# Expert sums on TensorE in four 64x64 tiles, two picks at a time, in a two-layer model on one core

## Chip, cores and metric

One of the eight cores of a Trainium2 chip runs the whole program. The metric is the time of one execution in microseconds (us) on the device. TensorE multiplies into PSUM, which has 8 banks of 128 partitions x 512 fp32 numbers; VectorE (DVE), ScalarE (ACT) and GpSimd (POOL) do the rest, and SyncE (SP) issues the stream of weights.

## What is computed

Two blocks over 512 tokens of width 1024. The first has windowed attention and a convolution branch, then PEER: for each token, 8 heads pick 16 of 16384 experts each, and

```python
s_top, i_top = lax.top_k(s, PEER_TOPK)          # per head and key half, then over the 16x16 sums
g = jax.nn.softmax(best, axis=-1)
ue = jnp.take(u_tab, idx, axis=0)               # idx: token, head, pick
ve = jnp.take(v_tab, idx, axis=0)
act = jax.nn.gelu(jnp.einsum('thkd,td->thk', ue, t), approximate=False)
return jnp.einsum('thk,thkd->td', (g * act), ve)
```

So 128 experts are summed for each token, and each has a row of 1024 for the dot product and a row of 1024 for the sum. The second block is two layers: an mLSTM mixer, attention over a memory of 256 rows and a squared-ReLU MLP of 4096; then a pooling mixer, attention and MLP again.

## The kernel before

**Tiles.** Activations lie transposed, features on partitions. A weight tile is 128 output features by 1024, 512 KB, streamed in a ring of four (`RING`). Each is split by ScalarE (`upper_after`) and VectorE (`lower_after`) into an upper and a lower part, and a product is 24 matmuls (three for each of 8 blocks of 128 features, L523 to L525), over 512 tokens or, in the mixer, attention and MLP of layer one, over a half of 256. `SECTIONS` gives for each section its first tile n and first product o.

**Banks.** Product o goes to PSUM bank o modulo 4. The reader of a product adds one to that bank's semaphore (`free`), and TensorE waits for it before product o + 4 (`wait_bank`). Banks 4 and 5 hold sums of squares, means, scores and turned values of the moment; banks 6 and 7 hold the expert sums.

**Picks.** A pick p is one expert for each of 128 tokens; there are 128 picks for each of 4 token blocks, 512 in all. GpSimd gathers its 128 rows of 8 KB (both rows of the expert) into one of up to ten slots (L492); VectorE takes the dot product (`expert_dot`, L2053); ScalarE makes the weight and from it a 128x128 diagonal matrix (`expert_weight`, L1342 to L1351), of which there are two; TensorE multiplies the diagonal with the gathered rows, in fp32, in two halves of 512 columns (`expert_sum`, L771), adding to banks 6 and 7, and frees the slot (`pick_used`). After 128 picks ScalarE copies the two banks out (L1357), TensorE turns them by 8 transposes (`turn_peer`, L780) and VectorE adds them to the residual (`add_peer`, L2062); the next block's first pick waits for that.

**Order.** All engines follow one order that is written out. The first 256 picks (`EARLY`) come with only the memory's 16 products between them. The others are spread over the tiles of the first half: `pick_ends` gives for each tile the number of picks that TensorE has added after it (two a tile, and some more at gaps), and `groups` names the places where several products are computed together, feature block by feature block, with their picks behind them. VectorE's dots run up to two picks ahead (`dot_picks`); ScalarE weighs the picks of a tile before it reads that tile's product (`weigh_picks`).

**A head of the mixer** (`half_lstm_core`): scores (L888), two tiles (the output gate, copied out by ScalarE at L1407) with picks behind each, the denominator (L901, read at L2307), the floor (L906), two value products (L913, read at L2319). `lstm_out` begins four products of the output projection over six of eight feature blocks while the last head is normalised.

## Time and profile before

| | |
|---|---|
| median of 3 runs | 3343.65 us (3343.54 to 3348.61) |
| the profiled execution | 3350.57 us, its span 3348.8 us |
| TensorE busy | 2926.9 us (87%) |
| VectorE, ScalarE, GpSimd busy | 2245.0, 1396.0, 600.2 us |
| gathers (queue q0) | 536.90 MB, 512 picks |
| weight stream | 390 tiles of 512.0 KB |
| picks on TensorE | from 624.9 to 2274.1 us |

A busy TensorE is not TensorE at its peak: a matmul's record runs on while the next has begun, so the time of a matmul is read from start to start. The DMA share is the mean busy share of the core's 16 DMA engines; it can come out a little over one.

### The profile page before, as it was taken

Reading aid. Unit: us, or ns where it says so; the run is one execution under the profiler, and the core shown is the slowest. Engines: PE = TensorE matmul, PEld = TensorE weight load, DVE = VectorE, ACT = ScalarE, POOL = GpSimd, SP = SyncE. Lnnn points to the kernel's source line nnn. Section 1 sums busy time; section 2 is a strip of 40 time slices with the busy share of each in tenths; the row PEclk is TensorE's granted clock in tenths of the full one; section 3 lists DMA queues with packets and bytes.
Section 4 is the critical chain, followed back from the end, with each engine's and each line's share of the span. In section 5 each row is a group of like instructions: output and inputs, shape, how many; then the busy total and the mean of one; then the engine's idle time right before and its main releaser. Section 6 shows DMA issues by size and latency. Waiting matters only on the chain. (4 is left out here: it accounts for less than half of the span.)

```text
span 3348.8 us, 40044 instructions
## 1 busy us (share of the span) xinstructions
PE 2926.9 (87%) x13452; PEld 2098.1 (63%) x13452; DVE 2245.0 (67%) x4588; ACT 1396.0 (42%) x2972; POOL 600.2 (18%) x545
## 2 busy tenths in 40 slices
PE   6999899877888888888889899997888976989998
PEld 6777677422344443556556566666778974778886
DVE  6775554588878886755666776777667777564445
ACT  3346323333444443655444544445544433332222
POOL 0000000233333444331323233330000011000000
PEclk9999899988898898998989999998989987989999
DMA  6531122799999999896868799992224540122221
GB/s 243 197 109 63 38 88 82 281 370 387 384 384 388 414 419 404 333 371 218 319 255 349 309 418 419 418 415 82 87 94 140 189 145 19 57 82 94 92 97 51
DMA packets 142422, 779.05 MB, mean 233 GB/s; under 512 B 15008, under 2 KB 18208, under 8 KB 76448
## 3 DMA queue, kind: packets, MB, share of 16 engines
q0 software_dynamic: 73728, 536.90, 39.8%
q1 hardware_dynamic: 62832, 220.43, 18.8%
q10 hardware_dynamic: 5680, 19.40, 1.6%
q8 instruction: 101, 1.65, 0.2%
q14 instruction: 81, 0.66, 0.1%
HBM read 774.58 MB, written 2.10 MB: 232 GB/s over the span
## 5 line engine op out<-in xcount | busy, mean ns | idle before, releaser
L492 POOL DMA_INDIRECT slots<-in_experts,consts x376 | 419.0, 1114 | 1371.4 <-PE psum L771 725.8
L2053 DVE SCALAR_TENSOR_TENSOR slots<-slots,work 128x1024 f32<-128x1024 f32 x376 | 460.5, 1225 | 236.1 <-DMA slots<-in_experts,consts 217.4
L1685 DVE TENSOR_TENSOR wlo<-w,whi 128x1024 fp32r<-128x1024 f32 x390 | 473.7, 1220 | 140.6 <-ACT whi L1151 139.4
L771 PE MATMUL psum<-slots,acc 128*128 128x512 f32 x824 | 420.6, 663 | 114.6 <-ACT acc L1351 114.6
L1151 ACT ACTIVATE whi<-w 128x1024 fp32r<-128x1024 f32 x390 | 409.1, 1050 | 212.8 <-PE psum L525 212.0
L771 PEld LDWEIGHTS psum<-slots,acc 128*128 128x128 f32 x824 | 167.5, 211 | 351.6 <-issue 188.8
L771 PE MATMUL psum<-slots,consts 128*128 128x512 f32 x680 | 324.9, 622 | 29.8 <-ACT consts L1351 27.2
L1342 ACT ACTIVATE consts<-consts 128x1 f32<-128x1 f32 x512 | 100.8, 197 | 473.5 <-DVE slots L2053 356.6
L523 PE MATMUL psum<-xhi,whi 128*128 128x512 f32 x664 | 268.5, 404 | 1.9 <-DVE wlo L1685 1.9
L523 PE MATMUL psum<-xhi_h,whi 128*128 128x256 f32 x880 | 267.8, 304 | 2.0 <-DVE wlo L1685 2.0
L524 PE MATMUL psum<-xlo,whi 128*128 128x512 f32 x664 | 262.9, 396 | 0.0
L525 PE MATMUL psum<-xhi,wlo 128*128 128x512 f32 x664 | 262.8, 396 | 0.0
L524 PE MATMUL psum<-xlo_h,whi 128*128 128x256 f32 x880 | 248.0, 282 | 0.0
L525 PE MATMUL psum<-xhi_h,wlo 128*128 128x256 f32 x880 | 247.7, 281 | 0.0
L771 PEld LDWEIGHTS psum<-slots,consts 128*128 128x128 f32 x680 | 126.7, 199 | 176.1 <-issue 121.9
L523 PE MATMUL psum<-yhi_h,whi 128*128 128x256 f32 x640 | 195.2, 305 | 4.0 <-DVE ylo_h L2366 4.0
L523 PE MATMUL psum<-yhi,whi 128*128 128x512 f32 (+1 forms) x416 | 170.3, 409 | 31.4 <-POOL ylo L510 21.8
L524 PE MATMUL psum<-ylo_h,whi 128*128 128x256 f32 x640 | 179.3, 280 | 0.0
L525 PE MATMUL psum<-yhi_h,wlo 128*128 128x256 f32 x640 | 179.2, 280 | 0.0
L523 PEld LDWEIGHTS psum<-xhi_h,whi 128*128 128x128 f32 x880 | 168.3, 191 | 12.1 <-issue 7.2
L524 PEld LDWEIGHTS psum<-xlo_h,whi 128*128 128x128 f32 x880 | 168.1, 191 | 9.7 <-issue 9.6
L525 PEld LDWEIGHTS psum<-xhi_h,wlo 128*128 128x128 f32 x880 | 167.9, 191 | 0.0
(336 smaller groups left out, 5884.8 us busy)
## 6 DMA issues: line engine op xcount, KB each, us to landing
w<-in_stream SPq DMA_DIRECT2D x390, 512.0 KB
arena<-in_wmod SPq DMA_DIRECT2D x4, 2048.0 KB, 17.8
arena<-in_wmod ACTq DMA_DIRECT2D x8, 1024.0 KB, 6.7
acc<-in_wmod ACTq DMA_DIRECT2D x8, 1024.0 KB, 8.0
slots<-in_experts,consts POOLq DMA_INDIRECT x376
xres<-in_xT SPq DMA_DIRECT2D x1, 2048.0 KB, 15.1
outT<-xres SPq DMA_DIRECT2D x8, 256.0 KB, 2.0
arena<-in_experts,consts POOLq DMA_INDIRECT x93
```

The lines of the kernel that those rows point to most:

```text
L492: pool.indirect_dma_start(out=slots[slot], out_offset=None, in_=a["experts"], in_offset=bass.IndirectOffsetOnAxis(ap=indices[:, p:p + 1], ...
L523: pe.matmul(dst, hi, xh(k), start=(j == 0), stop=False)
L524: pe.matmul(dst, hi, xl(k), start=False, stop=False)
L525: mm = pe.matmul(dst, lo, xh(k), start=False, stop=(j == len(ks) - 1))
L771: mm = pe.matmul(bank(6 + half), diag(p), v[:, half * T:(half + 1) * T], start=(c == 0), stop=(c == PICKS - 1))
L1151: act.activation(whi[:, s, :, :].rearrange("p k n -> p (k n)"), w32[:, s, :], ACT.Copy)\
L1342: act.activation(gelus[:, c:c + 1], inner[:, c:c + 1], ACT.Gelu).then_inc(sem("gelu_ready"), 1)
L1685: dve.tensor_tensor(wlo[:, s, :, :].rearrange("p k n -> p (k n)"), w32[:, s, :], whi[:, s, :, :].rearrange("p k n -> p (k n)").bitcast(F32 ...
L2053: dve.scalar_tensor_tensor(u, u, 1.0, tokens[:, p // PICKS, :], ALU.mult, ALU.mult, accum_out=inner[:, c:c + 1]).then_inc(sem("dotted"), 1)
```

## The change

Two picks are added together, by eight fp32 matmuls over 64 rows and 64 columns of the array. The diagonal is 128x64 (rows 0 to 63 hold the weights of tokens 0 to 63 on its diagonal, rows 64 to 127 those of the others), and there are four of them. An even pick sends token rows 0 to 63 to PSUM partitions 0 to 63 and rows 64 to 127 to partitions 64 to 127; an odd pick crosses them. Row group r and half h go to bank 4 + 2r + h, so the sums take four banks, and the crossed parts are brought together when the block is turned: 16 fp32 matmuls with two identities of 64 stacked (`pair`) in place of 8 transposes, behind four copies.

Since banks 4 to 7 are taken, the products from the memory's keys up to the second half's mixer use banks 0 and 1 alone (`out_banks`), and what was in banks 4 and 5 goes to 2 and 3 in that time (`side`, `norm_bank`). In the first half, groups of four products become groups of two, and two products of the output projection are begun early, not four. Elsewhere `bank(o % RING)` becomes `out_bank(o)`, the same bank as before. The core of the diff:

```diff
+def out_banks():
+
+    first, last = SECTIONS["memk"][1], SECTIONS["lstm1"][1]
+    banks = [o % (2 if first <= o < last else RING) for o in range(len(DONE))]
+    return banks, [banks[:o].count(b) for o, b in enumerate(banks)]
+
+
+OUT_BANK, OUT_TURN = out_banks()
...
-    groups = {first: 2, SECTIONS["xq0"][0]: 4, SECTIONS["mlp0"][0]: 4}
+    groups = {first: 2, SECTIONS["xq0"][0]: 2, SECTIONS["mlp0"][0]: 2}
...
-        diags = [t.rearrange("p (a n) -> p a n", a=2)
+        diags = [t.rearrange("p (a n) -> p a n", a=4)
                  for t in (flat_acc[:, 512:768], consts[:, _CONST["perm"][0]:_CONST["perm"][0] + 256])]
 
         def diag(p):
-            return diags[p // EARLY][:, p % 2, :]
+            return diags[p // EARLY][:, p % 4, :]
 
...
+        def out_bank(o):
+            return bank(OUT_BANK[o])
+
+        def side(half):
+            return 2 if half == 0 else 4
+
+        def norm_bank(ni):
+            return 2 if 3 <= ni < 7 else 4
...
-            if o >= RING:
-                eng.wait_ge(bank_free[o % RING], o // RING + shift)
+            if OUT_TURN[o]:
+                eng.wait_ge(bank_free[OUT_BANK[o]], OUT_TURN[o] + shift)
...
-                if c == 0:
+                if p % 2 == 0:
+                    return
+                if c == 1:
                     pe.wait_ge(sem("peer_added"), 8 * t) if t else pe.wait_ge(sem("tokens_copied"), 2 * TT)
-                if p == 0:
+                if p == 1:
                     pe.wait_ge(sem("key_scores_copied"), HP)
                 pe.wait_ge(sem("diagonal"), p + 1)
-                v = slots[SLOT[p]][:, D:2 * D]
                 for half in range(2):
-                    mm = pe.matmul(bank(6 + half), diag(p), v[:, half * T:(half + 1) * T], start=(c == 0),
-                                   stop=(c == PICKS - 1))
-                mm.then_inc(sem("pick_used"), 1)
+                    f = slice(D + half * T, D + (half + 1) * T)
+                    for q in (p - 1, p):
+                        for r in range(2):
+                            rows = slice(64 * r, 64 * r + 64)
+                            to = 64 * (r ^ (q % 2))
+                            mm = pe.matmul(psum[to:to + 64, 4 + 2 * r + half, :], diag(q)[rows, :], slots[SLOT[q]][rows, f],
+                                           start=(c == 1), stop=(c == PICKS - 1))
+                        if half:
+                            mm.then_inc(sem("pick_used"), 1)
 
             def turn_peer(t):
 
+                pe.wait_ge(sem("peer_copied"), 4 * t + 4)
                 for half in range(2):
-                    pe.wait_ge(sem("peer_copied"), 2 * t + half + 1)
                     for k in range(4):
-                        mm = pe.transpose(bank(6 + half)[:, k * P:(k + 1) * P],
-                                          peer_tokens(t)[:, half, k * P:(k + 1) * P], ident)
+                        for r in range(2):
+                            f = (4 * half + k) * P
+                            c = k * P + 64 * r
+                            mm = pe.matmul(bank(6 + half)[:, c:c + 64], peer_tokens(t)[:, r, f:f + P], const("pair"),
+                                           start=True, stop=True)
                     mm.then_inc(sem("peer_turned"), 1)
 
-            def turn_copied(m, o, src, tiles, turned):
+            def turn_copied(m, o, src, tiles, turned, at=2):
...
-                lstm_out(0, range(0, 6))
-                lstm_out(1, range(0, 6))
+                begun = 2 * (1 + half)
+                for m in range(begun // 2):
+                    lstm_out(m, range(0, 6))
                 head_sums(3)
-                lstm_out(2, range(0, 6))
+                for m in range(begun // 2, begun - half):
+                    lstm_out(m, range(0, 6))
                 head_spread(3)
-                lstm_out(3, range(0, 6))
-                for m in range(4):
+                for m in range(begun - half, begun):
+                    lstm_out(m, range(0, 6))
+                for m in range(begun):
                     lstm_out(m, range(6, 8))
-                for m in range(4, KB):
...
-                half_linear_group(n, range(o, o + 4), (sem(f"split{4 + 4 * half}"), 0))
+                group = 4 if half else 2
+                half_linear_group(n, range(o, o + group), (sem(f"split{4 + 4 * half}"), 0))
+                sum_picks(n + 1)
                 for m in range(KB):
-                    if m >= 4:
+                    if m >= group:
                         half_linear(n + m, o + m + (0, 0, 0, 0, 1, 1, 2, 2)[m])
...
-                half_linear_group(n, range(o, o + 4), (sem(f"split{5 + 4 * half}"), 0))
-                sum_picks(n + 3)
+                group = 4 if half else 2
+                half_linear_group(n, range(o, o + group), (sem(f"split{5 + 4 * half}"), 0))
+                sum_picks(n + 1)
+                for m in range(group, 4):
...
-                if p >= 2:
-                    act.wait_ge(sem("pick_used"), p - 1)
-                act.activation(diag(p), ident, ACT.Copy, scale=weights[:, c:c + 1])\
+                if p >= 4:
+                    act.wait_ge(sem("pick_used"), p - 3)
+                act.activation(diag(p), const("pair"), ACT.Copy, scale=weights[:, c:c + 1])\
...
                 act.wait_ge(sem("pick_used"), PICKS * (t + 1))
-                for half in range(2):
-                    act.activation(peer_tokens(t)[:, half, :], bank(6 + half), ACT.Copy).then_inc(sem("peer_copied"), 1)
-
-            def turn_back(m, dst, tiles, turned):
+                for r in range(2):
+                    for half in range(2):
+                        act.activation(peer_tokens(t)[:, r, half * T:(half + 1) * T], bank(4 + 2 * r + half), ACT.Copy)\
...
+    parts["pair"] = np.tile(np.eye(64), (2, 1))
```

## Rows read from the trace of the kernel before

**Rows 1.** The page: the span, and the DMA share in 40 slices.

```profile
span 3348.8 us, 40044 instructions
...
DMA  6531122799999999896868799992224540122221
```

**Rows 2.** Windows of the three parts: busy us (count) per engine, clock, DMA share, GB/s.

```profile
625.00:1330.00 705.00, 567.50 (x1432) 258.09 (x1432) 568.88 (x1527) 291.04 (x898) 282.85 (x256) 0.90 0.98 394
1330.00:1925.00 595.00, 515.18 (x2283) 340.15 (x2284) 379.61 (x735) 307.32 (x716) 166.87 (x146) 0.92 0.79 308
1925.00:2275.00 350.00, 345.40 (x1737) 232.45 (x1735) 243.25 (x389) 159.56 (x411) 115.20 (x104) 0.99 0.98 404
```

**Rows 3.** Timeline, TensorE, one MLP tile: start us, duration us, engine, line, what.

```profile
1990.23 0.68 PE L523 MATMUL psum<-xhi_h,whi 128*128 128x256 f32 x1
...
1990.75 0.28 PE L524 MATMUL psum<-xlo_h,whi 128*128 128x256 f32 x1
...
1993.43 3.59 PE L771 MATMUL psum<-slots,consts 128*128 128x512 f32 x8
...
1996.46 0.68 PE L523 MATMUL psum<-xhi_h,whi 128*128 128x256 f32 x1
```

**Rows 4.** Windows in the middle part with a full DMA share, three of five.

```profile
1400.00:1425.00 25.00, 24.93 (x128) 17.06 (x127) 20.54 (x41) 21.26 (x39) 7.65 (x8) 1.00 1.02 419
...
1450.00:1500.00 50.00, 47.30 (x226) 30.11 (x224) 24.41 (x36) 24.21 (x69) 19.41 (x18) 1.00 0.99 395
...
1800.00:1850.00 50.00, 43.59 (x195) 26.72 (x194) 32.27 (x61) 20.68 (x55) 17.84 (x17) 1.00 1.00 405
```

**Rows 5.** Waits of 1925 to 2275: who waited for whom, total, times, longest.

```profile
POOL slots L492 <- PE psum L771: 136.7, 64, 3.8
...
DVE slots L2053 <- DMA slots<-in_experts,consts: 60.8, 42, 2.0
```

**Rows 6.** Timeline, TensorE, attention values (64 output rows) and the product behind.

```profile
141.22 1.09 PE L682 MATMUL psum<-arena 128*64 128x128 f32 x8
142.24 0.50 PE L523 MATMUL psum<-xhi,whi 128*128 128x512 f32 x1
142.57 0.39 PE L524 MATMUL psum<-xlo,whi 128*128 128x512 f32 x1
142.80 0.40 PE L525 MATMUL psum<-xhi,wlo 128*128 128x512 f32 x1
```

**Rows 7.** Timeline of one head of the mixer; in brackets idle time and releaser.

```profile
1528.26 6.68 PE L771 MATMUL psum<-slots,consts 128*128 128x512 f32 x8 [3.51 <-ACT consts L1351]
...
1542.67 0.82 PE L901 MATMUL psum<-work,consts 128*128 128x256 f32 x4
...
1544.64 0.38 ACT L1407 ACTIVATE arena<-psum 128x256 f32<-128x256 f32 x1 [3.84 <-DVE ylo_h L1693]
...
1546.16 0.42 DVE L2307 COPY work<-psum 128x256 f32<-128x256 f32 x1
...
1546.28 0.38 ACT L1407 ACTIVATE arena<-psum 128x256 f32<-128x256 f32 x1 [0.31 <-DVE ylo_h L1693]
...
1546.92 1.98 PE L913 MATMUL psum<-work,arena 128*128 128x256 f32 x8
...
1549.38 0.88 DVE L2319 TENSOR_TENSOR acc<-psum,work 128x256 f32<-128x256 f32 x2
...
1549.97 1.65 PE L888 MATMUL psum<-arena 128*128 128x256 f32 x4
```

**Rows 8.** Timeline at the cross attention's start: scores, VectorE's read, picks.

```profile
1694.18 1.99 PE L955 MATMUL psum<-arena 128*128 128x256 f32 x8 [0.64 <-ACT arena L1407]
...
1696.21 0.42 DVE L2342 TENSOR_REDUCE small<-psum 128x1 f32<-128x256 f32 x1 [7.24 <-PE psum L955]
...
1702.19 3.78 PE L771 MATMUL psum<-acc,consts 128*128 128x512 f32 x4 [6.01 <-ACT consts L1351]
```

**Rows 9.** Timeline: turning a block's sum (TensorE), copying one out (ScalarE).

```profile
1330.50 1.15 PE L780 MATMUL psum<-consts,arena 128*128 128x128 f32 x8 [0.69 <-ACT arena L1357]
...
1845.78 1.09 ACT L1357 ACTIVATE slots<-psum 128x512 f32<-128x512 f32 x2 [2.07 <-PE psum L771]
```

More of the change, by code:

```diff
@@ L535, in linear @@
                 wait_bank(pe, o)
-                feature_product(bank(o % RING)[:, 0:cols], n % RING, XH, XL, range(KB), ready=ready,
+                feature_product(out_bank(o)[:, 0:cols], n % RING, XH, XL, range(KB), ready=ready,
                                 last_sem=tile_done)
@@ L843, in half_lstm_in @@
                     if m > 9:
-                        turn_copied(m - 10, o + 9, wh, HT, turned)
-                turn_copied(7, o + 9, wh, HT, turned)
+                        turn_copied(m - 10, o + 9, wh, HT, turned, side(half))
+                turn_copied(7, o + 9, wh, HT, turned, side(half))
                 pe.wait_ge(sem("values_copied"), turned + 8)
@@ L848, in half_lstm_in @@
                 for t in range(HT):
-                    mm = pe.transpose(bank(4)[:, 4 * t:4 * t + 4], arow[:, t * P:(t + 1) * P],
+                    mm = pe.transpose(bank(side(half))[:, 4 * t:4 * t + 4], arow[:, t * P:(t + 1) * P],
                                       const("ident", 4)[:, 0:4])
@@ L863, in head_sums @@
                         for j in range(2):
-                            mm = pe.matmul(bank(4)[:, c:c + 1], wh[:, j, c * P:(c + 1) * P], ones[:, 0:1],
+                            mm = pe.matmul(bank(side(half))[:, c:c + 1], wh[:, j, c * P:(c + 1) * P], ones[:, 0:1],
                                            start=(j == 0), stop=(j == 1))
@@ L870, in head_spread @@
                     pe.wait_ge(sem("floor_read"), 4 * half + h + 1)
-                    spread(bank(5), stats[0][:, 0:4], H).then_inc(sem("head_inverse_spread"), 1)
+                    spread(bank(side(half) + 1), stats[0][:, 0:4], H).then_inc(sem("head_inverse_spread"), 1)
                 for h in range(4):
@@ L882, in half_lstm_core @@
                         pe.wait_ge(sem("head_rms_read"), 4 * half + h - 1)
-                    pe.matmul(bank(4)[:, 0:H], pick, mrow, start=True, stop=True).then_inc(sem("max_spread"), 1)
+                    pe.matmul(bank(side(half))[:, 0:H], pick, mrow, start=True, stop=True).then_inc(sem("max_spread"), 1)
                     for j in range(firsts):
@@ L905, in half_lstm_core @@
                         pe.wait_ge(sem("lstm_split"), 8 * half + 2 * h)
-                    pe.matmul(bank(5)[:, 0:H], pick, frow, start=True, stop=True).then_inc(sem("floor_spread"), 1)
+                    pe.matmul(bank(side(half) + 1)[:, 0:H], pick, frow, start=True, stop=True).then_inc(sem("floor_spread"), 1)
                     for j in range(2):
@@ L954, in x_scores @@
                         for j in range(2):
-                            mm = pe.matmul(bank(4)[:, t * CT:(t + 1) * CT], xq_h[:, 2 * h + j, t * P:(t + 1) * P],
+                            mm = pe.matmul(bank(side(half))[:, t * CT:(t + 1) * CT], xq_h[:, 2 * h + j, t * P:(t + 1) * P],
                                            mk[:, 2 * h + j, :], start=(j == 0), stop=(j == 1))
@@ L964, in x_turn @@
                         for j in range(2):
-                            mm = pe.transpose(bank(5)[:, H * j + t * P:H * j + (t + 1) * P],
+                            mm = pe.transpose(bank(side(half) + 1)[:, H * j + t * P:H * j + (t + 1) * P],
                                               xp_h[:, t, j * P:(j + 1) * P], ident)
@@ L1204, in copy_product @@
                 wait_product(act, o)
-                free(act.activation(dst, bank(o % RING)[:, 0:cols], func, **more), o)
+                free(act.activation(dst, out_bank(o)[:, 0:cols], func, **more), o)
             def raw(i, o):
@@ L1476, in half_lstm_in @@
                     if m:
-                        turn_back(m - 1, lv[:, HT * half:HT * half + HT, :], HT, turned)
+                        turn_back(m - 1, lv[:, HT * half:HT * half + HT, :], HT, turned, side(half))
                 act.wait_ge(sem("floor_arg"), half + 1)
@@ L1529, in x_copy @@
                         half_product(x_half_value_out(half, h - 1))
-                    act.activation(xpT_h.rearrange("p j n -> p (j n)"), bank(5), ACT.Copy)\
+                    act.activation(xpT_h.rearrange("p j n -> p (j n)"), bank(side(half) + 1), ACT.Copy)\
                         .then_inc(sem("x_turned_copied"), 1)
@@ L2122, in half_product @@
                 wait_product(dve, o)
[L2123 removed]
+                return out_bank(o)
             def half_wait_read(o):
@@ L2240, in head_stats @@
                     dve.wait_ge(sem("head_rms"), 4 * half + h + 1)
-                    dve.tensor_scalar(st, bank(4)[:, 0:HT], 1.0 / 256, LN_EPS, ALU.mult, ALU.add)\
+                    dve.tensor_scalar(st, bank(side(half))[:, 0:HT], 1.0 / 256, LN_EPS, ALU.mult, ALU.add)\
                         .then_inc(sem("head_rms_read"), 1)
@@ L2250, in head_out @@
                         t = acc_h[:, 2 * h + j, :]
-                        step(dve.tensor_tensor(t, t, bank(5)[:, 0:H], ALU.mult))
+                        step(dve.tensor_tensor(t, t, bank(side(half) + 1)[:, 0:H], ALU.mult))
                         step.settle()
@@ L2311, in half_lstm_core @@
                     step.settle()
-                    dve.tensor_tensor(den, den, bank(5)[:, 0:H], ALU.max).then_inc(sem("floor_read"), 1)
+                    dve.tensor_tensor(den, den, bank(side(half) + 1)[:, 0:H], ALU.max).then_inc(sem("floor_read"), 1)
                     dve.wait_ge(sem("floor_read"), 4 * half + h + 1)
@@ L2339, in x_softmax_in @@
                             dve.wait_ge(sem("x_turned"), i - 1)
-                        s = bank(4)[:, t * CT:(t + 1) * CT]
+                        s = bank(side(half))[:, t * CT:(t + 1) * CT]
                         mx = small[:, 40 + t:41 + t]
```

108 lines of the change are left out of this document (55 added, 53 removed).

## The prediction

> **What bounds the kernel now.** I read the page first: its span against the time, then the DMA share slice by slice [rows 1]. It stands at 9 tenths from slice 8 to 15 and again from slice 23 to 26. That is the stretch in which 512 picks are gathered, so I asked for the three parts of it by window [rows 2]: the picks with nothing but memory products between them (625 to 1330 us), the first half's mixers (1330 to 1925 us) and the first half's MLP (1925 to 2275 us). The reader is to see DMA shares of 0.98, 0.79 and 0.98. The first and the third part are held by the transfers; only the middle one has room, 0.79 at 308 GB/s.
>
> What TensorE pays per pick is read from one tile of the MLP in order of time [rows 3]. A tile's 24 products start at 1990.23, its two picks at 1993.43, the next tile at 1996.46: 6.23 us. Eight records belong to two picks, and a pick issues two matmuls, so every fp32 matmul of 512 columns is two records. From 1990.75 to 1993.43 the 23 remaining products take 2.68 us, 0.117 each, 2.80 for 24; so the picks take 6.23 - 2.80 = 3.43 us, 0.43 a record, 1.72 us a pick. A tile moves 0.52 MB of weights and two gathers of 1.05 MB, 2.62 MB; in 6.23 us that is 421 GB/s, what the busiest windows of the part before show (419, [rows 4]). So in the MLP both are full at once. The waits of that part say the same [rows 5]: the gathers' queue waits for TensorE to free a slot (136.7 us in the largest group), and VectorE waits for gathered rows (60.8 us). Who gets faster alone there gains nothing.
>
> **The change part by part.**
>
> *The picks on TensorE.* Two picks now issue 16 matmul records in place of 8 (two halves, two picks, two row groups, two records each), each over 64 rows and 64 columns and still 512 columns long. No row shows two records of different tiles of the array side by side, so the price lies between two bounds made of the 0.43 us of a record: one after another 16 x 0.43 = 6.88 us a pair, twice today's 3.44; with two under way at a time 3.44; with four, 1.72. The order in which they stand puts four different tiles behind each other, and they write disjoint pairs of bank and partitions, so nothing in the code holds them apart. I take four, 1.72 us a pair, 0.86 saved a pick, and keep both other values as rivals. The Trainium skill, in TensorEngine Tiling (Array Packing), Key Properties, says that different tiles can load weights and multiply in parallel; no row of this kernel shows it, and by it the sum is the one I take.
>
> *Changing the array's mode.* Products use all 128 rows and picks 64, so each run of picks has a change ahead and one behind. Rows show one such change [rows 6]: behind products of 64 output rows the first product of 512 columns takes from 142.24 to 142.57, 0.33 us, the next to 142.80, 0.23. So 0.1 us a change, 0.2 for the picks between two tiles. For changes between other shapes I take the same, with three times it as the upper bound. Between pairs that follow each other there is none.
>
> *Where the saving counts.* In 625 to 1330 the DMA share is 0.98: a pair's TensorE work falls from 3.44 to 1.72 us, but a pair already has 705 / 128 = 5.5 us. Nothing is gained. In the MLP the DMA is full: nothing either, and the 0.2 us of mode changes lie under the 1.72 saved. In 1330 to 1925 the windows with a share of 0.99 and more [rows 4] are five: 1400 to 1425 and two like it at 419 GB/s (1625 to 1675, 1900 to 1925), 1450 to 1500 and 1800 to 1850. They make 200 us and 81.9 MB (100 x 419 + 50 x 395 + 50 x 405). The part carries 595 x 308 = 183.3 MB. The other 395 us carry 101.4 MB, at 2.62 MB a tile 39 tiles with 78 picks. There TensorE sets the pace: 78 x 0.86 = 67 us saved, less 39 x 0.2 = 8 of mode changes: 59. The bound on the other side: at 419 GB/s 183.3 MB need 437 us, so the part can't lose more than 158.
>
> *Two banks for the first half's products.* I looked for who is late in one head of the mixer [rows 7]. The denominator's product (L901, 1542.67) must now wait for the first gate's copy, which starts at 1544.64 and takes 0.38: ready at 1545.02. But VectorE reads it only at 1546.16, after the head's output, and the floor's product waits for that too; the first value product starts at 1546.92, and its new bank is freed at 1546.66. The next scores (1549.97) need the first value read, VectorE from 1549.38: free at 1549.8. Each is just in time, so I take nothing, with 1 us a head, 4 us, as the other bound. In plain sections ScalarE or VectorE has to read product m before it can prepare the picks after m+1 or m+2, and TensorE's order has these picks ahead of product m+2: nothing.
>
> *Groups of two.* At the cross attention's start four products run by k, then the scores, then picks. Rows show what that costs now [rows 8]: the scores run at 1694.18, VectorE has idled 7.24 us when it reads them, and the picks follow at 1702.19, TensorE having idled 6.01 us. With two in the group, four picks stand ahead of the scores. That may gain some us; the two products that are no longer under the norm cost 2.8 us each. I set it at nothing. The output projection has two products of 18 records begun early instead of four: 2 x 18 x 0.117 = 4 us lost.
>
> *Turning the sums.* A token block's sum is now copied out in four pieces, all of them ahead of the first turn, and turned by 16 fp32 matmuls of 64 columns instead of 8 transposes. The two copies are 1.09 us and the 8 turns 1.15 us [rows 9]; two copies more are 1.1, and twice as many matmuls, of half the columns and twice the records, cost about one to two of these more. Some 2.5 us each, on the path at 1330 and 1846 only, where the next picks wait for it: 5.
>
> *Slots.* A pair's first slot is held until the second pick has its diagonal, 2.75 us longer (705 / 256). With six to nine slots that takes a little from the gathers under way in 625 to 1330: 4 us, between 0 and 12. ScalarE's smaller diagonal (64 columns) and four of them instead of two work the other way.
>
> Sum: -67 + 8 + 4 + 5 + 4 = -46 us; with a us given back to waits that the picks now cover, -45. The profiled execution took 3350.6 us (span 3348.8), so 3305.6; it stands 6.9 over the median of the runs, 3343.65, and from there 3299.
>
> **The rivals.**
>
> *Two at a time (slower).* A matmul's two records share a tile, so the second must wait for the first, 0.43 us. If TensorE starts its records strictly in their order, the next tile's first record can't pass it: it starts beside it. Then exactly two run together, and 16 records take 8 x 0.43 = 3.44 us, no less than today, with a tail of 0.43 before a full-array product can start and 0.2 of mode changes: 4.07 against 3.44, 0.63 a pair. In the MLP, full on TensorE already, 64 tiles lose 40; in the middle 64 pairs, of which the busy share of 515 / 595 counts, lose some 35; with the 13 of the small terms 88 us: 3343.65 + 88 = 3432. It decides on one point: whether a record of another tile can start while the one ahead of it waits. For it speaks that the records of now stand strictly one behind the other, 0.43 apart [rows 3]; but they all use the whole array, so they would in either case. The Trainium skill, in TensorE: Matmul & The Clock Gate, The mechanism, says that matmuls start and end strictly in program order; this rival is what that rule does with two records to a matmul. No row here shows it on tiles.
>
> *One after another (far slower).* 6.88 us a pair: 3.44 more for each of the 128 pairs after 1330, 440 us, and 1.4 more than the 5.5 of a pair in the first 705 us, 128 x 1.4 = 176. Some 3950.
>
> *Faster on TensorE, and no faster.* The time goes to VectorE and ScalarE or to late gathers. TensorE waited for the diagonals in the head above (3.51 us before L771 at 1528.26, [rows 7]), and shorter sums make that wait longer; a TensorE that idles more may be granted less clock (0.90 and 0.92 in the parts in which it idled, 0.99 in the MLP, [rows 2]), and the products pay for it: those 8 records took 6.68 us behind the idle time, against 3.59 in the MLP [rows 3, 7]. Then the 59 shrink to some 15, and the small terms of 13 take it: within 7 us of 3344. From about 45 lost in this way the change is slower.
>
> **How the numbers follow.** Four at a time, with its gain: 0.51. Two at a time: 0.32. Faster on TensorE and no faster in all: 0.12. One after another: 0.05. The predicted time is the likeliest, 3299; its own range is 3260 to 3330 (the saving may also reach into the full windows, and the picks at the lower clock save more than 0.86; or half of it is covered). The range of all reaches to two at a time, from 3260 to 3440. The measurement can't tell less than 0.2%, 6.7 us, from no change. Faster by more: 0.49 (nearly all of the first case, a little of the third). Within: 0.09. Slower: 0.42.
>
> **What the profile after would show.** Right: the records of the picks start four within 0.43 us, a pair takes under 2 us between products, and 1330 to 1925 shrinks by some 45 us with a DMA share near 0.86, while 625 to 1330 and the MLP keep their length. Wrong in the second way: a pair takes about 4 us, an MLP tile 6.9 instead of 6.23, and the DMA share there falls to 0.92. Wrong in the third: a pair of about 7 us. If bank waits matter, VectorE or ScalarE stands as releaser before L901 and L913. The two places where I am least sure are the number of tiles under way and how much of the 59 us the waits for diagonals take back.

## The result, and the profile after

The changed kernel took 3386.53 us, the median of 3 runs (3377.25 to 3391.74), against 3343.65 before: a ratio of 1.0119, with an interval of 1.0081 to 1.0157. It is slower by 43 us, where faster by 45 was forecast. Its profiled execution took 3386.53 us, its span 3384.7.

Here are the span, the granted clock and the DMA share in 40 slices, from the page of the changed kernel; they answer to [rows 1].

```profile
span 3384.7 us, 44341 instructions
...
PEclk9999799776677777798888799997989996989999
DMA  6532122788899999797788799993224650123331
```

The same three parts as in [rows 2], by window: length, busy time and instructions of TensorE, its weight loads, VectorE, ScalarE and GpSimd, then the granted clock, the DMA share and GB/s.

```profile
625.00:1330.00 705.00, 390.11 (x2364) 143.97 (x2368) 553.00 (x1500) 271.21 (x861) 254.51 (x241) 0.73 0.94 372
1330.00:1925.00 595.00, 439.36 (x2812) 278.70 (x2804) 372.78 (x723) 301.23 (x722) 182.08 (x149) 0.82 0.79 312
1925.00:2300.00 375.00, 298.06 (x2377) 203.63 (x2377) 264.57 (x426) 166.53 (x444) 116.34 (x116) 0.99 1.00 412
```

The reader is to see that TensorE is busy for less of both of the first parts, as intended, and that the first part has lost what it lived on: its DMA share is 0.94 where it was 0.98, and its clock has fallen too.

One tile of the MLP in order of time, start and length, answers to [rows 3]: 24 products, a pair of picks, the next product.

```profile
2009.80 0.39 PE L543 MATMUL psum<-yhi_h,whi 128*128 128x256 f32 x1
...
2014.16 0.65 PE L797 MATMUL psum<-acc,consts 64*64 64x512 f32 x2 [1.26 <-ACT consts L1387]
2014.17 0.65 PE L797 MATMUL psum<-arena,consts 64*64 64x512 f32 x2
2014.64 0.59 PE L797 MATMUL psum<-acc,consts 64*64 64x512 f32 x2
2014.65 0.60 PE L797 MATMUL psum<-arena,consts 64*64 64x512 f32 x2
2015.07 0.59 PE L797 MATMUL psum<-acc,consts 64*64 64x512 f32 x2
2015.08 0.60 PE L797 MATMUL psum<-arena,consts 64*64 64x512 f32 x2
2015.50 0.60 PE L797 MATMUL psum<-acc,consts 64*64 64x512 f32 x2
2015.51 0.60 PE L797 MATMUL psum<-arena,consts 64*64 64x512 f32 x2
2016.04 0.39 PE L543 MATMUL psum<-yhi_h,whi 128*128 128x256 f32 x1
2016.26 0.28 PE L544 MATMUL psum<-ylo_h,whi 128*128 128x256 f32 x1
2016.38 0.28 PE L545 MATMUL psum<-yhi_h,wlo 128*128 128x256 f32 x1
```

Sixteen records start in four groups of four, each group within 0.02 us, the groups 0.43 to 0.48 apart. Two of each four belong to either pick (their operands lie in acc and in arena), so they are four different matmuls, and the group behind them holds the second records. Four tiles work at a time: from the pair's first record to the next product are 2016.04 - 2014.16 = 1.88 us. The engine waits in another place: 1.26 us for the diagonal, where it had not idled. The tile is as long as before, 2016.04 - 2009.80 = 6.24 us.

The full price of a pair, to be set beside the 3.43 us of [rows 3], is read where no idle time stands ahead of it:

```profile
1927.70 0.28 PE L545 MATMUL psum<-xhi_h,wlo 128*128 128x256 f32 x1
1927.91 1.95 PE L797 MATMUL psum<-slots,consts 64*64 64x512 f32 x16
1929.79 0.38 PE L543 MATMUL psum<-xhi_h,whi 128*128 128x256 f32 x1
1930.01 0.28 PE L544 MATMUL psum<-xlo_h,whi 128*128 128x256 f32 x1
```

From the last product ahead of the pair to the second behind it are 2.31 us; less two products of 0.117, the pair and both changes of the array's mode take 2.08 us.

What follows needs a ledger of where the time goes. The four turns of the sums (L780 before, L810 after) cut the span into five stages. The first column is when the first turn starts, the others are the stages' lengths, each from its first turning record to the next turn's, the last to the span's end; in us, from the profiled executions. The last column is the median over that of the kernel before on the same chip. A profiled execution can stand up to 12 us off its kernel's median (3361.22 for 3349.34 in single4_pairs), so differences of a few us between stages say little.

| kernel | first turn | 2nd | 3rd | 4th | rest | against before |
|---|---|---|---|---|---|---|
| before | 987.8 | 342.7 | 515.9 | 429.0 | 1073.4 | |
| the change | 1013.5 | 356.8 | 504.7 | 431.5 | 1078.3 | +43 |
| the change, run again | 1010.0 | 354.9 | 502.1 | 431.5 | 1079.7 | +39.7 |
| hold | 1009.5 | 348.6 | 529.2 | 432.2 | 1072.9 | +47.8 |
| banks_only | 988.6 | 340.1 | 501.9 | 428.4 | 1073.5 | -9.6 |
| fast_turn | 1015.1 | 352.2 | 497.0 | 426.3 | 1072.2 | +19.9 |
| fill | 1014.9 | 351.4 | 502.5 | 431.5 | 1075.3 | +38.5 |
| single4 | 973.2 | 340.1 | 486.2 | 427.0 | 1080.3 | -34.7 |
| single4_hold | 998.1 | 344.0 | 495.5 | 426.8 | 1070.9 | -5.2 |
| single4_pairs | 1001.2 | 345.7 | 505.1 | 425.8 | 1081.5 | +6.5 |
| single4_late | 1015.0 | 348.6 | 506.7 | 427.9 | 1081.4 | +31.6 |
| single4_fill | 981.3 | 339.6 | 489.3 | 427.0 | 1073.7 | -29.9 |
| single4_groups | 977.2 | 339.5 | 482.5 | 425.4 | 1076.6 | -43.5 |
| single4_banks | 974.6 | 339.7 | 476.1 | 424.6 | 1073.0 | -49.3 |

In the profiled execution of the change 26 us are lost before the first turn and 14 more before the second, both in the part that I had put down as untouched; 11 are won in the third stage, where I had expected most of the gain. The rest varies between 1071 and 1081 over all kernels, in no order that I can read.

The window from 625 us to before's first turn is compared in all kernels; it holds the sums of the first 128 picks, or most of them, and in single4 and its kin a few more. The kernel before and then the changed one:

```profile
625.00:988.00 363.00, 279.87 (x610) 119.12 (x611) 289.49 (x798) 141.33 (x439) 138.73 (x129) 0.88 0.97 383
```

```profile
625.00:988.00 363.00, 178.19 (x1016) 52.82 (x1016) 272.07 (x764) 124.78 (x406) 126.12 (x120) 0.70 0.90 353
```

GpSimd has 9 instructions fewer behind it, 120 for 129, and the bytes fall from 363 x 383 = 139.0 MB to 128.1: 10.4 gathers of 1.05 MB, at 2.75 us a pick 29 us, about what the first turn is late. So the time is lost in the gathers. How many slots they have is in the code of all kernels (`SLOT_OPENS`): six for picks 0 to 55, seven to 119, eight to 183, nine to 255, and six again from pick 256 on. Two theories say why the gathers are late. *Slots*: the sums come two at a time, so the even pick's slot is held until the odd one has its diagonal. *Clock*: TensorE idles more and is granted less (0.70 for 0.88), and what hangs on it runs later.

### The profile page after: what moved, and what is told of

Read it like the earlier page. It is cut to its first block and busy times, and to the rows that moved or that the text cites. A ratio compares the mean times of both kernels' runs of the same rounds, so it can differ in the third digit from the quotient of the medians.

```text
span 3384.7 us, 44341 instructions
## 1 busy us (share of the span) xinstructions
PE 2638.7 (78%) x15596; PEld 1903.9 (56%) x15596; DVE 2244.5 (66%) x4588; ACT 1378.9 (41%) x2981; POOL 588.1 (17%) x545
## 5 line engine op out<-in xcount | busy, mean ns | idle before, releaser
L797 PE MATMUL psum<-slots,acc 64*64 64x512 f32 x1648 | 331.8, 849 | 291.7 <-ACT acc L1387 289.5
L797 PEld LDWEIGHTS psum<-slots,acc 64*64 64x64 f32 x1648 | 84.0, 184 | 488.8 <-ACT acc L1387 355.8
L797 PE MATMUL psum<-slots,consts 64*64 64x512 f32 x1360 | 187.0, 670 | 110.9 <-ACT consts L1387 109.5
L544 PE MATMUL psum<-xlo_h,whi 128*128 128x256 f32 x912 | 259.1, 284 | 0.0
L545 PE MATMUL psum<-xhi_h,wlo 128*128 128x256 f32 x912 | 258.3, 283 | 0.0
L543 PEld LDWEIGHTS psum<-xhi_h,whi 128*128 128x128 f32 x912 | 176.5, 193 | 40.7 <-issue 24.9
L543 PE MATMUL psum<-yhi,whi 128*128 128x512 f32 (+1 forms) x416 | 170.3, 409 | 31.3 <-POOL ylo L530 21.7
L543 PE MATMUL psum<-yhi_h,whi 128*128 128x256 f32 x640 | 184.9, 289 | 4.0 <-DVE ylo_h L2404 4.0
L544 PEld LDWEIGHTS psum<-xlo_h,whi 128*128 128x128 f32 x912 | 176.4, 193 | 0.1
L545 PEld LDWEIGHTS psum<-xhi_h,wlo 128*128 128x128 f32 x912 | 175.9, 193 | 0.0
L544 PE MATMUL psum<-ylo,whi 128*128 128x512 f32 (+1 forms) x416 | 167.5, 403 | 0.0
```

Source lines behind the costliest of these rows:

```text
L543: pe.matmul(dst, hi, xh(k), start=(j == 0), stop=False)
L544: pe.matmul(dst, hi, xl(k), start=False, stop=False)
L545: mm = pe.matmul(dst, lo, xh(k), start=False, stop=(j == len(ks) - 1))
L797: mm = pe.matmul(psum[to:to + 64, 4 + 2 * r + half, :], diag(q)[rows, :], slots[SLOT[q]][rows, f], start=(c == 1), stop=(c == PICKS - 1))
```

## Experiments

### The wait alone, the sums alone, the turn alone, the clock alone

**hold** is the kernel before with one number changed: a gather waits for an even pick's slot as if that were freed with the odd one.

```diff
-                    pool.wait_ge(sem("pick_used"), q + 1)
+                    pool.wait_ge(sem("pick_used"), q + 1 if q % 2 else q + 2)
```

> The kernel before, and only the release of a slot is later: the gather that reuses an even pick's slot waits for the odd pick behind it too, as in the change. Slot theory (a pair's first slot is held until the second pick is summed, so fewer gathers are under way while few slots exist): the first 128 picks take about 20 us longer than 363 us (625 to 988), the whole is 20 to 35 us slower. Clock theory (TensorE idles more, is granted 1.2 GHz, and frees the slots late): nothing changes here, as TensorE has the same work, so within 5 us of the kernel before.

**single4** is the kernel before with the change's sums, but pick by pick: row group r and half h of a pick go to bank 6 + r, partitions from 64 (r xor h). So the four tiles of one pick differ, two banks are enough, and nothing crosses between picks. The turn is that of before, behind four copies that put the halves in place.

```diff
-                    mm = pe.matmul(bank(6 + half), diag(p), v[:, half * T:(half + 1) * T], start=(c == 0),
-                                   stop=(c == PICKS - 1))
+                    f = slice(D + half * T, D + (half + 1) * T)
+                    for r in range(2):
+                        rows, to = slice(64 * r, 64 * r + 64), 64 * (r ^ half)
+                        mm = pe.matmul(psum[to:to + 64, 6 + r, :], diag(p)[rows, :], slots[SLOT[p]][rows, f],
+                                       start=(c == 0), stop=(c == PICKS - 1))
...
-                    act.activation(peer_tokens(t)[:, half, :], bank(6 + half), ACT.Copy).then_inc(sem("peer_copied"), 1)
+                    for r in range(2):
+                        at = 64 * (r ^ half)
+                        act.activation(peer_tokens(t)[64 * r:64 * r + 64, half, :], psum[at:at + 64, 6 + r, :], ACT.Copy)\
+                            .then_inc(sem("peer_copied"), 1)
```

> The kernel before, four 64x64 tiles for one pick alone: its left half of the row goes through the two straight tiles, its right half through the two crossed ones, row group r writes bank 6 + r, so two banks suffice, products keep four, and the turning stays with 8 transposes behind four copies of 64 partitions. Nothing is held for a pair. Slot theory: no loss in 625 to 1330, and the middle part gains 30 to 60 us: 3285 to 3320. Clock theory: the early picks run at 1.2 GHz with 1.72 us each, as long as the full array needs at 2.4, so about 0 in 625 to 1330 and the same gain behind it. If both are wrong and tiles themselves cost, it is as slow as the change, 3380.

**fast_turn** is the change with 8 transposes in place of the 16 fp32 matmuls of the turn. It leaves out the crossed half of the sums.

```diff
-                        for r in range(2):
-                            f = (4 * half + k) * P
-                            c = k * P + 64 * r
-                            mm = pe.matmul(bank(6 + half)[:, c:c + 64], peer_tokens(t)[:, r, f:f + P], const("pair"),
-                                           start=True, stop=True)
+                        f = (4 * half + k) * P
+                        mm = pe.transpose(bank(6 + half)[:, k * P:(k + 1) * P], peer_tokens(t)[:, 0, f:f + P], ident)
```

> The changed kernel with 8 transposes of the straight sums in place of 16 fp32 matmuls of both (so half of each sum is left out of the output). The turn took 5.4 to 7.1 us in the changed kernel, 1.15 before. If all of that is on the path at each of the four blocks: 18 to 24 us faster than the change, 3362 to 3368. If only at the last two or three: 10 to 15 us.

**fill** is the change with four matmuls behind each of the first 78 pairs that nobody reads, to keep TensorE's clock up.

```diff
+                if p < 156:
+                    for _ in range(4):
+                        pe.matmul(bank(3)[:, 0:256], ident, consts[:, 0:256], start=True, stop=True)
```

> The changed kernel with four more fp32 matmuls of 256 columns into an unused bank behind each of the first 78 pairs (1.7 us at 2.4 GHz), whose results nobody reads, so that TensorE is about as busy as before. Clock theory: the granted clock in 625 to 988 rises from 0.70 to about 0.88, pairs shorten from about 3 to 1.75 us, and most of the 26 us lost up to the first turn come back: about 3365. Slot theory: the clock rises, the 26 us stay or grow: 3385 or more.

The kernel before took 3342.38 us beside these. Measured: hold 3390.14 (1.0135, 1.0118 to 1.0152), single4 3307.65 (0.9886, 0.9866 to 0.9907), fast_turn 3362.33 (1.0056, 1.0033 to 1.008), fill 3380.87 (1.0116, 1.0097 to 1.0134).

The wait alone costs 48 us, more than the whole change and more than the 20 to 35 that I expected of it. Single4 lies in the range of the slot theory, and fast_turn in the range for a turn that is on the path at all four blocks. Fill lies 4 us under the slot theory's 3385 and 16 over the clock theory's 3365. The window of hold, then that of fill:

```profile
625.00:988.00 363.00, 264.14 (x554) 108.81 (x554) 275.83 (x772) 131.67 (x411) 128.14 (x121) 0.88 0.91 358
```

```profile
625.00:988.00 363.00, 264.88 (x1488) 132.44 (x1488) 271.37 (x764) 123.68 (x405) 126.77 (x120) 0.87 0.89 352
```

Hold has the clock of before, 0.88, and the gathers of the change: a DMA share of 0.91, 358 GB/s. Fill has the clock of before too, 0.87, and its first turn is where it was, at 1014.9 for 1013.5. So the loss ahead of the first turn is there with the clock (hold) and stays when the clock is given back (fill).

What the hold does is in the chain of waits over 625 to 988 us (who waits at which line for whom: us in total, times, longest). Before, hold, the change:

```profile
DVE slots L2053 <- DMA slots<-in_experts,consts: 46.9, 29, 4.9
```

```profile
DVE slots L2053 <- DMA slots<-in_experts,consts: 69.8, 40, 5.7
```

```profile
PE psum L797 <- ACT acc L1387: 184.0, 32, 8.7
DVE slots L2091 <- DMA slots<-in_experts,consts: 74.0, 42, 6.1
```

VectorE waits longer for gathered rows, 46.9, then 69.8 and 74.0 us. The one engine that got faster, TensorE, only waits longer for its diagonals: 184.0 us, where before it was 88.0 (35 times).

Single4 has all of the faster sums and no hold. It is 35 us faster than before, and it runs at the low clock:

```profile
625.00:988.00 363.00, 206.91 (x1180) 61.86 (x1172) 300.11 (x834) 142.09 (x454) 142.78 (x132) 0.70 0.98 392
```

Its share is 0.98 at 392 GB/s: the part that I had called full could carry more than 383 once the slots came free sooner. The kernel before shows it too: in its own second stage (987.8 to 1330.5 us), with eight and nine slots, it moves 405 GB/s.

The turn in the change, and in fast_turn, each with the product behind it (start, length, engine and line; in brackets the idle time before it and what ended it):

```profile
1013.45 6.78 PE L810 MATMUL psum<-consts,arena 128*128 128x64 f32 x32 [2.73 <-ACT arena L1394]
1019.99 0.56 PE L543 MATMUL psum<-mem_hi,whi 128*128 128x256 f32 x1
```

```profile
1015.07 1.09 PE L808 MATMUL psum<-consts,arena 128*128 128x128 f32 x8 [2.22 <-ACT arena L1391]
1015.92 0.36 PE L543 MATMUL psum<-mem_hi,whi 128*128 128x256 f32 x1
```

It is 6.54 us for 0.85, but not at the same clock: the granted clock was 0.52 from 1013.5 to 1020 us in the change and 1.00 in the turn of fast_turn. Fill has the change's turn at a granted clock of 1.00:

```profile
1014.93 3.79 PE L813 MATMUL psum<-consts,arena 128*128 128x64 f32 x32 [0.29 <-ACT arena L1397]
1018.53 0.36 PE L543 MATMUL psum<-mem_hi,whi 128*128 128x256 f32 x1
```

There it takes 3.60 us, 0.11 a record, and 8 transposes at the lower level take 1.76 (1864.26 us in fast_turn, clock 0.50), 0.21 a record. So at either level a record of 64 columns costs what a transpose of 128 does, and there are 32 for 8. The stages behind the turns are 4.6, 7.7, 5.2 and 6.1 us shorter in fast_turn.

### The banks alone, and the hold on top of the new sums

**change_again** is the changed kernel once more, to have it beside the others.

> The changed kernel once more, so that the three beside it are compared with it on one chip. About 3385.

**banks_only** is the change with the sums, diagonals, copies and turn of before. The products still use banks 0 and 1, the groups are of two and two products are begun early.

```diff
-                    for q in (p - 1, p):
-                        for r in range(2):
-                            rows = slice(64 * r, 64 * r + 64)
-                            to = 64 * (r ^ (q % 2))
...
+                    mm = pe.matmul(bank(6 + half), diag(p), v[:, half * T:(half + 1) * T], start=(c == 0),
+                                   stop=(c == PICKS - 1))
```

> The changed kernel with the sums of the kernel before (one full-array matmul per half, two diagonals, banks 6 and 7, 8 transposes): what is left of the change is two banks for the first half's products, groups of two and two products begun early. By the prediction's own terms it costs 4 us, give or take 10. If the banks hid a cost of their own, it is 15 us or more slower than the kernel before; if the groups of two pay for themselves, it is up to 10 faster.

**single4_hold** is single4 with the one number of hold.

> Four tiles for one pick, and only the release of an even pick's slot waits for the odd pick. Slot theory: the 47 us that the same wait cost without tiles come back, somewhat less as the odd pick is now summed in half the time: 3340 to 3360, and with the 24 us of the turn that is the change's time. If the change were slow because of how its 16 matmuls lie (pairs, crossing, four banks), this kernel keeps most of its gain, below 3325.

**single4_groups** is single4 with the change's groups of two in the cross attention and the MLP, on the banks of before.

> Four tiles for one pick with the change's groups of two at the first half's cross attention and MLP, on four banks. At the start of the cross attention the gathers then begin again earlier: 0 to 10 us faster than four tiles alone (3308), if the products that are no longer under the norm cost less than that; otherwise up to 6 us slower.

Beside a before of 3343.68: change_again 3383.40 (1.0124, 1.0107 to 1.0141), banks_only 3334.08 (0.9971, 0.9954 to 0.9987), single4_hold 3338.43 (0.9989, 0.9975 to 1.0002), single4_groups 3300.19 (0.9870, 0.9852 to 0.9888).

The hold costs 29 us on top of single4 (from -34.7 to -5.2), less than on the kernel before and just under the range expected, and takes nearly all of its gain. The DMA share of single4_hold in the window is 0.94:

```profile
625.00:988.00 363.00, 198.75 (x1080) 54.63 (x1080) 285.23 (x788) 133.27 (x426) 136.09 (x124) 0.69 0.94 371
```

But 29 us do not carry single4 to the change: at the same low clock its share is 0.94 for 0.90 and its first turn at 998 for 1013. Banks and groups are not what is missing. They gained 10 us, 14 in the third stage, where I had expected nothing or a loss. Something else of the pair had to cost more.

### What else a pair does to the slots

**single4_pairs** is single4 with both picks' matmuls issued after the odd diagonal; each pick still frees its slot behind its own.

```diff
+                if p % 2 == 0:
+                    return
...
+                for q in (p - 1, p):
...
+                    mm.then_inc(sem("pick_used"), 1)
```

> Four tiles, two banks, cheap turning, but TensorE adds both picks of a pair only when the second has its diagonal, as the change does (each pick still through all four tiles by itself). Slot theory: the first turn starts 8 to 15 us after that of single4_hold (998), as the even pick's sum now stands between the odd pick's diagonal and its release too: 3345 to 3360. If something else in the change's form costs (its four banks, its crossing of picks, its slow turn), the first turn stays at 998 and the whole at 3338.

**single4_fill** is single4 with two matmuls that nobody reads behind each of the first 128 picks.

> Four tiles for one pick, and behind each of the first 128 picks two fp32 matmuls of 256 columns into an unused bank, read by nobody, 0.87 us at 2.4 GHz. Clock theory: the clock of 625 to 988 rises from 0.70 to about 0.87 and the first turn comes 5 us or more before 973. Slot theory: the clock rises and the first turn moves by less than 3 us, or gets later by what the extra matmuls take in bursts.

**single4_late** is single4_pairs with the even pick's slot freed as in the change: in the order of issue behind 12 of the pair's 16 records, and not behind 8.

```diff
+                for q in (p - 1, p):
...
+                        if q == p:
+                            mm.then_inc(sem("pick_used"), 1)
```

> single4_pairs with the even pick's slot released not when its own 8 records are done but after 12 of the pair's 16, where the change releases it. The change's first turn starts 9 to 12 us after that of single4_pairs (1001). Slot theory: this small delay, 0.9 us at the full clock and up to 1.7 at the lower, makes up a good part of it, first turn 1003 to 1010, the whole 3352 to 3365. If the first turn stays at 1001, the rest of the change's first part has another cause, which stays open.

**single4_banks** is single4's sums on the banks, groups and early products of the change.

> Four tiles for one pick on the change's banks and groups (two banks for the first half's products, groups of two, two products begun early). banks_only gained 10 us over the kernel before, single4_groups 7 over single4. If the banks themselves cost nothing, 3295 to 3303, the same as single4_groups; if two banks cost once the picks are shorter, above 3306.

The first two ran beside a before of 3342.89: single4_pairs 3349.34 (1.0018, 1.0 to 1.0036), single4_fill 3313.01 (0.9912, 0.988 to 0.9944). The last two beside 3340.8: single4_late 3372.44 (1.0093, 1.0069 to 1.0116), single4_banks 3291.46 (0.9856, 0.983 to 0.9882). The windows of single4_pairs and of single4_late:

```profile
625.00:988.00 363.00, 185.09 (x1072) 57.36 (x1072) 283.07 (x785) 131.45 (x424) 131.58 (x124) 0.71 0.94 369
```

```profile
625.00:988.00 363.00, 178.79 (x1016) 53.43 (x1016) 271.67 (x764) 125.15 (x405) 125.98 (x120) 0.71 0.90 353
```

With this the change's first part is reproduced without its four banks, its crossing and its turn. Adding both picks behind the odd diagonal costs 12 us more than the wait of a gather alone (from -5.2 to +6.5). Its first turn, at 1001, came earlier than I had expected. These 12 us are the difference of two medians from two chips, each known to 5 or 6. Freeing the even slot behind the odd pick's left half costs 25 more (to +31.6), more than I had expected. At the low clock the groups of four records stand 0.85 to 0.91 us apart (in the change L797 at 1698.44, 1699.35, 1700.20 and 1701.05). By the order of issue 4 records are one such group, but the second records of the odd pick's four matmuls all stand in the pair's last group, so the release comes two groups later, 1.7 us. The updates of `pick_used` in the traces show it: one pair is released at 709.04 and 710.74 us in single4_pairs, one at 700.39 and 700.45 in single4_late, one at 1702.14 and 1702.20 in the change. So in the change both slots of a pair come free together, behind all 16 records. With that the window is the change's own, 0.90 and 353 GB/s, and so is the first turn, 1015.0. ScalarE waits for the same semaphore before it overwrites a diagonal, so a later release could also act through the diagonals; no run parts the two, but over 625 to 988 us ScalarE waits only 8.9 us there in single4_late, and 1.8 in single4_pairs.

Single4_banks came out 4 us under the range expected: two banks cost nothing with the shorter sums either.

Single4_fill raised the clock of the same window to 0.93 and was not faster: its first turn is 8 us later than single4's, 981 for 973. The filler costs something itself, so what it could win back under its own cost, some 8 us, stays open.

## Why the prediction was wrong

**The step that failed** is the one called *Slots*: "4 us, between 0 and 12". It measured 48 alone on the kernel before, and with the new sums 29 for the wait, 12 for the pairing and 25 for the later release, 66 in all. The 4 stood there without a working. I had read a DMA share of 0.98 [rows 2] as a stretch that is held by the transfers, and took the slots for a reserve. But GpSimd waits for TensorE to free a slot in that very part: over 625 to 988 us of the kernel before that wait is the largest. I had read it for the MLP alone [rows 5].

```profile
POOL slots L492 <- PE psum L771: 202.0, 99, 8.2
```

So ahead of the first turn the rate is slots divided by the time that each is kept. The size there could have been had from numbers that stood in the prediction. A slot comes round every six or seven picks of 2.75 us, 16.5 to 19.3 us. Half of the slots held 2.75 us longer make 1.4 us on the mean, 7.1 to 8.3% of that. Over the 363 us that is an estimate of 26 to 30; hold moved 358 GB/s for 383, 6.5% less, and lost 21.7. The same estimate for the second stage, with eight and nine slots, gives 19 to 21 us, but hold lost only 5.9 there: the DMA share was 1.00 before and 0.99 in hold, so there the transfers did set the rate. The other part that I had not looked at is the third stage, with six slots again: hold lost 13.3 us in it.

**Four tiles at a time** was right: groups of four records 0.43 us apart at the full clock, four to a pair, 1.72 us. The rival *two at a time*, 4.07 a pair, and *one after another* are refuted by the changed kernel's own records: the first record of the next tile starts beside one whose second record still waits. I had set a rule of the Trainium skill (TensorE: Matmul & The Clock Gate, The mechanism) against the forecast, that matmuls start and end strictly in program order. The trace agrees with it as far as matmuls go: within each group the records start in the order of issue, 0.007 us apart. What fails is my step from matmuls to their records: the second records of all four tiles start together, 0.43 to 0.48 behind four first ones.

**The mode change** was forecast at 0.1 us, 0.2 a pair. A pair between two products takes 2.08 us where its four groups are 1.72, so the two changes cost 0.36 together, within the upper bound. At 39 tiles that is 6 us more than forecast.

**The saving in the middle** was right in kind and half in size. The prediction had 59 us net in 1330 to 1925. Single4, which has nothing against it, won 29.7 in the third stage (it ends at 1846 us, 79 before the forecast's stretch does; the fourth won 2.0). The waits show where more than the rest can have gone. From 1340 to 1840 us TensorE waits for diagonals, before and then in single4:

```profile
PE psum L771 <- ACT consts L1351: 37.5, 20, 6.0
```

```profile
PE psum L773 <- ACT consts L1353: 83.1, 45, 6.0
```

That is 46 us of faster sums turned into waiting (39.3 and 84.8 us over each kernel's own third stage). This was the first half of the rival *faster on TensorE, and no faster*, and it holds in part. Its second half is the clock of that stage, which fell from 0.92 to 0.85 in single4; no run raised it there. By the records it is small: at the lower level are 58 of single4's 256 groups of sums, 0.43 us more each, where before 47 of 512 records were, and 179 records of products where 161 were, 0.095 more each. That makes an estimate of 7 us of TensorE's time.

**The first part**, "nothing is gained", was wrong twice. The change lost 40 us there up to the second turn. Single4 won 17 there (14.6 and 2.6), with a DMA share of 0.98. A pick's sums are two groups of four records in place of four records, and its slot is free sooner; that this is the reason follows from the runs with a later release, it was not tried alone.

**The turn** was forecast at +5, at two places, 2.5 us each, of which 1.1 were for two more copies. Its matmuls alone measured 20 (39.7 - 19.9, each against before; the four stages behind a turn give 24 by the profiles); the copies, four in 2.06 us for two in 1.09, came out as forecast. I had put the 16 matmuls at one to two times the eight transposes more. They are 32 records, each as dear as a transpose at the same clock, so four times as much, and the lower clock doubles it: the change's four turns kept TensorE busy for 5.8 to 7.1 us, at a granted clock of 0.50 to 0.59, 26.2 in all where four turns like fill's first are 14.4. So of the turn's cost an estimate of 12 us is the clock's. And I had counted two places of four; the work behind all four turns came later.

**Banks and groups**, forecast at 0 and +4 for the products begun early, are -10. I did not trace which of the edits wins it; single4_groups gives 9 with the groups alone, on top of single4, and single4_banks 15 with all of them (from -34.7 to -49.3).

**The MLP** kept its 429 us (431.5, and 426.3 with the fast turn), as forecast: the DMA share is 1.00 from 1925 to 2300 us, and VectorE waits for gathered rows as before (68.7 us in the fourth stage before, 65.5 in the change).

The measured terms, added: single4 -34.7, wait +29.5, pairing +11.7, late release +25.1, turn +19.8, banks and groups -9.6. Their sum is +41.8; the change measured +39.7 in the run beside them and +42.9 in the first. That they meet so closely is in part luck: each difference is known to 5 to 8 us, and the turn and the banks were measured on other kernels than the four in front. With the banks as single4_banks has them, -14.6, the sum is +36.8.

The best version, single4_banks, takes 3291.46 us, 1.4% under the kernel before. It keeps the four tiles, the banks and the groups, and gives up the pairing.

## What to carry to other kernels

When a consumer is batched, every buffer of the batch is held until the last one's inputs are there. If the producer waits for buffers, price that as extra hold divided by the time that a buffer takes to come round, times the length of the stretch, even where the DMA share reads 0.97. Here that came out as an upper bound: 26 to 30 us where 21.7 were lost with six and seven slots, and 19 to 21 where 5.9 were lost with eight and nine, the transfers being at a share of 1.00. Count the buffers stretch by stretch. Ask what the batch is for: here four tiles needed four independent pieces, and a single pick had them, with row groups and halves crossed over two banks. A faster engine in front of a wait moves the wait, so read who is late next before multiplying the saving by its count.

## What the runs showed of the hardware

- Fp32 matmuls on 64x64 tiles overlap four at a time although each has two records: starts within 0.02 us in a group, 0.43 us between groups in the MLP, at the 2.4 GHz level, 0.85 where the engine had idled, at the 1.2 GHz level. A release issued behind one matmul of such a group comes with the whole group: 0.06 us between the two slots of a pair in the change, 1.7 in single4_pairs.
- Going from 128x128 products to 64x64 tiles and back cost 0.36 us together at the 2.4 GHz level (2.31 us between products, less 1.72 and 0.235).
- A DMA share of 0.97 at 383 GB/s was not the end of what the same gathers could move: single4_banks had 0.99 at 396 in the same window.
- A granted clock of 0.70 for 0.88 over 363 us did not keep single4 from being 35 us faster; the fillers that raised it to 0.87 and 0.93 won nothing clear.
- Records of fp32 matmuls with 128 rows and 64 moving columns took as long as transposes of 128 columns: 0.11 us at a granted clock of 1.00 (fill; fast_turn), 0.21 at 0.50 (the change; fast_turn's third turn). The matmul has two records, the transpose one.
- ScalarE copied 64x512 out of PSUM in 0.61 us (four in 2.44 in single4, two of them to the other 64 partitions), where 128x512 took 0.55 [rows 9]: half the partitions saved nothing.
